# Expert rows modulated before they are stored, fetched and turned one expert at a time; six early weight loads wait for the first rows

## What is computed

```python
x = x + gate1 * (merged @ w_out[l])
h2 = rmsnorm(x, norm2_g[l]) * (1.0 + scale2) + shift2
x = x + gate2 * grouped_moe(h2, router_w, router_b, w_gate[l], w_up[l], w_down[l])

def grouped_moe(h, router_w, router_b, w_gate, w_up, w_down):
    # 16 experts in 4 groups; every token goes to 2 experts of its best group
    hidden = silu(einsum('td,edf->tef', t, w_gate)) * einsum('td,edf->tef', t, w_up)
    hidden = hidden * combine[:, :, None]
    y = einsum('tef,efd->td', hidden, w_down)
```

## Time and profile before

| engine | busy us | share of the span |
|---|---|---|
| PE | 767.5 | 90% |
| DVE | 606.0 | 71% |
| ACT | 478.0 | 56% |
| POOL | 105.0 | 12% |

### The profile page before, as it was taken

The page is one execution under the profiler, slowest core; times in us unless marked ns, Lnnn a source line. Parts: engine busy times, 40 slices in busy tenths (PEclk is TensorE's granted clock), DMA queues, the critical chain, the costliest instruction groups (busy, mean ns, idle before and its releaser), DMA issues.

```text
span 854.4 us, 10046 instructions
## 1 busy us (share of the span) xinstructions
PE 767.5 (90%) x3628; PEld 592.9 (69%) x3628; DVE 606.0 (71%) x800; ACT 478.0 (56%) x618; POOL 105.0 (12%) x87
## 2 busy tenths in 40 slices
PE   3799999999999889999999729899999899999883
PEld 2687787776666556678888627677878787878772
DVE  4686887425998875545772427789899989898980
ACT  6334224455656335554235517769697869687750
POOL 4020000000000000010000110022324131313111
PEclk9799999999999999999999858999999999999996
DMA  9919993111031111153373695999999999999613
GB/s 286 316 51 373 390 390 128 50 50 51 1 99 49 50 50 51 50 173 99 99 280 140 216 375 171 341 311 377 359 376 355 383 375 339 371 340 373 220 25 53
DMA packets 86875, 183.35 MB, mean 215 GB/s; under 512 B 8064, under 2 KB 27624, under 8 KB 84784
## 3 DMA queue, kind: packets, MB, share of 16 engines
q1 hardware_dynamic: 79200, 156.29, 50.3%
q0 software_dynamic: 7632, 26.52, 11.1%
HBM read 170.17 MB, written 12.62 MB: 214 GB/s over the span
## 4 chain that ended last, share of the span: by engine, by line
PE 63%; ACT 10%; issue 8%; DVE 8%; DMA 7%; POOL 1%; SPq 1%; ACTq 0%; POOLq 0%; DVEq 0%
PE ps L646 16%; PE ps L647 15%; PE ps L648 15%; PE ps L802 4%; DMA gx<-rows_scratch,slot_tok 3%; ACT w_hi L1433 3%; ACT hgT_hi L1460 3%; DMA out<-ys,slot_tok 2%; ACT hm L1466 2%; DMA raw<-in_w_in 1%; PE ps L784 1%; PE ps L886 1%; DVE w_lo L1538 1%; PE ps L902 1%; PE ps L914 1%
## 5 line engine op out<-in xcount | busy, mean ns | idle before, releaser
L1858 DVE TENSOR_TENSOR w_lo<-raw,w_hi 128x2048 fp32r<-128x2048 f32 x80 | 179.7, 2285 | 15.9 <-ACT w_hi L1433 15.9
L1433 ACT ACTIVATE w_hi<-raw 128x2048 fp32r<-128x2048 f32 x80 | 151.0, 1910 | 12.0 <-PE ps L648 12.0
L646 PE MATMUL ps<-w_lo,hgT_hi 128*128 128x512 f32 x256 | 106.8, 417 | 15.0 <-DVE hgT_lo L1963 14.9
L646 PE MATMUL ps<-act_lo,w_hi 128*128 128x512 f32 x232 | 98.7, 426 | 7.1 <-DVE act_lo L1580 3.1
L647 PE MATMUL ps<-w_hi,hgT_lo 128*128 128x512 f32 x256 | 104.8, 409 | 0.0
L648 PE MATMUL ps<-w_hi,hgT_hi 128*128 128x512 f32 x256 | 104.2, 407 | 0.0
L648 PE MATMUL ps<-act_hi,w_hi 128*128 128x512 f32 x232 | 91.4, 394 | 0.0
L647 PE MATMUL ps<-act_hi,w_lo 128*128 128x512 f32 x232 | 91.1, 393 | 0.0
L1168 ACT ACTIVATE w_hi<-raw 128x2048 fp32r<-128x2048 f32 (+2 forms) x29 | 51.9, 1794 | 67.3 <-DMA raw<-in_w_in 44.1
L1538 DVE TENSOR_TENSOR w_lo<-raw,w_hi 128x2048 fp32r<-128x2048 f32 (+2 forms) x29 | 61.9, 2145 | 31.7 <-ACT w_hi L1168 31.5
L646 PEld LDWEIGHTS ps<-w_lo,hgT_hi 128*128 128x128 f32 x256 | 51.0, 199 | 28.9 <-DVE hgT_lo L1963 17.9
(11 more groups left out here) (266 smaller groups left out, 1418.8 us busy)
## 6 DMA issues: line engine op xcount, KB each, us to landing
raw<-in_w_down SPq DMA_DIRECT2D x32, 1024.0 KB, 10.6
raw<-in_w_gate SPq DMA_DIRECT2D x30, 1024.0 KB, 10.4
raw<-in_w_up SPq DMA_DIRECT2D x18, 1024.0 KB, 9.7
raw<-in_w_in SPq DMA_DIRECT2D x16, 1024.0 KB, 6.4
raw<-in_w_ada SPq DMA_DIRECT2D x16, 1024.0 KB, 7.1
raw_late<-in_w_up SPq DMA_DIRECT2D x14, 1024.0 KB, 8.6
raw<-in_w_ada SPq DMA_DIRECT2D x8, 512.0 KB, 6.8
raw_early<-in_w_ada SPq DMA_DIRECT2D x8, 512.0 KB, 6.2
```

Of the source, the lines that this page charges most:

```text
L646: pe.matmul(o, a[0], b[1], start=start, stop=False)
L1433: act.activation(e_hi[s_][:, :], e_raw[r][:, :], ACT.Copy).then_inc(e_top, 1)
L1858: dve.tensor_tensor(e_lo[s_][:, :], e_raw[r][:, :], e_hi[s_][:, :].bitcast(F32), ALU.subtract).then_inc(e_split, 1)
```

## The change

Five things change together.

1. DVE makes the fully modulated row before it is stored. POOL loads three broadcast rows (amp2r from scale2, shift2r, and g2r, which waits until PE is done with ob1). `amp_row` makes amp once, `by_amp` multiplies the new xres by it half by half, and `modulated` multiplies by 1/rms and adds the shift. ACT's `rows_scaled` goes. So after the transposes the high part is a plain copy, and the low part a subtraction: hm and nsh2c go.
2. Rows are turned for one expert at a time, in every stage, after the four chunks and before `down`: eight transposes, two ACT copies of 128x512, two DVE subtractions of 128x512. Every stage waits for its own two halves before chunks 0 and 1. Each of the two gx buffers has its own semaphore.
3. At the start only expert 0 is turned before stage 0, and its index is made by itself (`singly`) before that of expert 1.
4. The loads z = 6 to 11 wait, besides what they waited for, until expert 0's rows have landed.
5. In stage 15 the first half of `down(14)` runs before `turn_hid(15)` and the second half after it, and hidT is split in two halves.

```diff
+                    if isinstance(z, int) and 6 <= z < E_RAW:
+                        sp.wait_ge(rows_in[0], 16)
...
+            for dst, src in ((amp2r, mod_d[1][:, 0:D]), (shift2r, mod_d[0][:, D:2 * D])):
+                pool.dma_start(dst[:, :], src.partition_broadcast(P).rearrange("p a d -> p (a d)")).then_inc(ld_rw2, 16)
+            pool.wait_ge(seg_ready, seg_done("ob1", 3))
+            pool.dma_start(g2r[:, :], norm2_g.partition_broadcast(P).rearrange("p a d -> p (a d)")).then_inc(ld_rw2, 16)
...
-                pool.wait_ge(idx_ok, X - X % 2 + 2)
+                pool.wait_ge(idx_ok, X + 1)
                 if X >= 2:
-                    pool.wait_ge(hg_ps, 2 * (X - X % 2))
+                    pool.wait_ge(hg_ps, 2 * X - 2)
                 pool.indirect_dma_start(gx[X % 2][:, :], None, rows_d,
                                         bass.IndirectOffsetOnAxis(slot_tok[:, X % N_EXP:X % N_EXP + 1], 0)
-                                        ).then_inc(rows_in, 16)
+                                        ).then_inc(rows_in[X % 2], 16)
...
-            def turn_rows(X, units):
-
-
-                for u in units:
-                    if u == 0:
-                        pe.wait_ge(rows_in, 16 * X + 32)
-                    if not isinstance(X, int) or X > 0 or u >= 2:
-                        pe.wait_ge(hg_sp, 2 * X + u - 1)
-                    for j in range(2):
-                        kk = 2 * u + j
-                        for b in range(2):
-                            last = pe.transpose(ps[2 + u % 2][:, P * (2 * j + b):P * (2 * j + b) + P],
-                                                gx[b][:, P * kk:P * kk + P], ident[:, :])
+            def turn_rows(X, b):
+
+                pe.wait_ge(rows_in[b], 8 * X + 16 - 8 * b)
+                if not isinstance(X, int) or X > 0:
+                    pe.wait_ge(hg_sp, 2 * X)
+                for u in range(2):
+                    for j in range(4):
+                        kk = 4 * u + j
+                        last = pe.transpose(ps[2 + u][:, P * j:P * j + P], gx[b][:, P * kk:P * kk + P], ident[:, :])
                     last.then_inc(hg_ps, 1)
...
+                    if singly and b:
+                        pe.wait_ge(sel_ready, X + 2)
+                        pe.wait_ge(idx_ok, X + 1)
...
-                    pe.wait_ge(hg_sp, 2 * X + 2)
+                pe.wait_ge(hg_sp, 2 * X + 1)
                 if not fresh:
                     pe.wait_ge(silu_ok, X)
                 up_chunk(X, 0, b, z0, z)
-                if b == 0:
-                    pe.wait_ge(hg_sp, 2 * X + 4)
+                pe.wait_ge(hg_sp, 2 * X + 2)
...
-                if b == 1 and not last_:
-                    turn_rows(X + 1, (0, 1))
+                if last_:
+                    down(X - 1, z0 + 4, z + 4, (0,))
+                    turn_hid(X)
+                    down(X - 1, z0 + 4, z + 4, (1,))
+                    return
+                turn_rows(X + 1, 1 - b)
...
-            def rows_scaled(tt):
-                act.wait_ge(h2_rs, tt + 1)
-                act.activation(hn[:, tt, :], xres[:, tt, :], ACT.Copy, scale=st[:, tt, 5:6]).then_inc(h2_rows, 1)
...
-            def hg_high(X, u):
-                act.wait_ge(hg_ps, 2 * X + u + 1)
-                for j in range(2):
-                    kk = 2 * u + j
-                    last = act.activation(hgT_hi[:, :, kk, :], ps[2 + u % 2][:, 2 * P * j:2 * P * j + 2 * P].rearrange(
-                        "p (b s) -> p b s", b=2), ACT.Identity, bias=sh2c[:, kk:kk + 1], scale=amp2c[:, kk:kk + 1])
-                last.then_inc(hg_hi, 1)
-                act.wait_ge(hg_hi, 2 * X + u + 1)
-                for j in range(2):
-                    kk = 2 * u + j
-                    last = act.activation(hm[:, :, kk, :], hgT_hi[:, :, kk, :].bitcast(F32), ACT.Identity,
-                                          bias=nsh2c[:, kk:kk + 1])
-                last.then_inc(hg_hm, 1)
+            def hg_high(X, b):
+                for u in range(2):
+                    act.wait_ge(hg_ps, 2 * X + u + 1)
+                    act.activation(hgT_hi[:, b, 4 * u:4 * u + 4, :], ps[2 + u][:, :].rearrange("p (k s) -> p k s", k=4),
+                                   ACT.Copy).then_inc(hg_hi, 1)
...
+                if not last_:
+                    hg_high(X + 1, 1 - b)
...
+            def amp_row():
+                dve.wait_ge(ld_rw2, 48)
+                dve.scalar_tensor_tensor(out=amp2r[:, :], in0=amp2r[:, :], scalar=1.0, in1=g2r[:, :], op0=ALU.add,
+                                         op1=ALU.mult).then_inc(amp_ok, 1)
+                dve.wait_ge(amp_ok, 1)
+
+            def by_amp(half, t0, t1):
+
+                a = slice(512 * half, 512 * half + 512)
+                dve.wait_ge(x1_ready, 4 * half + t1)
+                dve.tensor_tensor(hn[:, t0:t1, a], xres[:, t0:t1, a],
+                                  amp2r[:, a].unsqueeze(1).broadcast_to([P, t1 - t0, 512]), ALU.mult).then_inc(rows_amp, 1)
+
+            def modulated(tt):
+                dve.wait_ge(rows_amp, 2 + tt)
+                dve.wait_ge(h2_rs, tt + 1)
+                dve.scalar_tensor_tensor(out=hn[:, tt, :], in0=hn[:, tt, :], scalar=st[:, tt, 5:6], in1=shift2r[:, :],
+                                         op0=ALU.mult, op1=ALU.add).then_inc(h2_rows, 1)
...
-            def hg_low(X, u):
-                dve.wait_ge(hg_hm, 2 * X + u + 1)
-                for j in range(2):
-                    kk = 2 * u + j
-                    last = dve.scalar_tensor_tensor(
-                        out=hgT_lo[:, :, kk, :], in0=ps[2 + u % 2][:, 2 * P * j:2 * P * j + 2 * P].rearrange(
-                            "p (b s) -> p b s", b=2), scalar=amp2c[:, kk:kk + 1], in1=hm[:, :, kk, :], op0=ALU.mult,
-                        op1=ALU.subtract)
-                last.then_inc(hg_sp, 1)
+            def hg_low(X, b):
+                for u in range(2):
+                    dve.wait_ge(hg_hi, 2 * X + u + 1)
+                    dve.tensor_tensor(hgT_lo[:, b, 4 * u:4 * u + 4, :], ps[2 + u][:, :].rearrange("p (k s) -> p k s", k=4),
+                                      hgT_hi[:, b, 4 * u:4 * u + 4, :].bitcast(F32), ALU.subtract).then_inc(hg_sp, 1)
...
+                if last_ is not None:
+                    dve.wait_ge(hidT_h, X + 1)
+                    dve.tensor_tensor(hidT_lo[:, 0:2, :], ps[4][:, 0:2 * P].rearrange("p (k s) -> p k s", k=2),
+                                      hidT_hi[:, 0:2, :].bitcast(F32), ALU.subtract).then_inc(hidT_sp, 1)
+                    dve.wait_ge(hidT_h2, last_)
+                    dve.tensor_tensor(hidT_lo[:, 2:4, :], ps[4][:, 2 * P:4 * P].rearrange("p (k s) -> p k s", k=2),
+                                      hidT_hi[:, 2:4, :].bitcast(F32), ALU.subtract).then_inc(hidT_sp2, 1)
+                    return
```

More of the change, by code:

```diff
@@ L184, in hybrid_layer @@
     before = tiny("before", [P])
[L185 to L186 removed]
+    sc2c, sh2c, g2c, amp2c = (at(n, [KD], F32, small[0] + i / 32)
+                                     for i, n in enumerate(("sc2c", "sh2c", "g2c", "amp2c")))
     identb = tiny("identb", [P], BF16)
@@ L1067, in slot_table @@
                                          start=(tt == 0), stop=(tt == NT - 1))
-                last.then_inc(ws_ps, 2)
+                    if singly:
+                        last.then_inc(ws_ps, 1)
+                if not singly:
+                    last.then_inc(ws_ps, 2)
             def up_chunk(X, cc, b, z0, z):
@@ L1079, in up_chunk, with down @@
                 m.then_inc(e_used, 1)
-            def down(X, z0, z):
-                pe.wait_ge(hidT_sp, X + 1)
-                if not isinstance(X, int) or X > 0:
-                    pe.wait_ge(y_sb, 2 * X)
-                for h in range(2):
+            def down(X, z0, z, halves=(0, 1), rest=None):
+                if 0 in halves:
+                    pe.wait_ge(hidT_sp, X + 1)
+                    if not isinstance(X, int) or X > 0:
+                        pe.wait_ge(y_sb, 2 * X)
+                for h in halves:
+                    if h and rest is not None:
+                        pe.wait_ge(hidT_sp2, rest)
                     pe.wait_ge(e_split, z + h + 1)
@@ L1128, in stage, with expert_pass @@
                     slot_table(X + 2, e + 2)
-            def expert_pass(X0):
-                slot_table(X0, 0)
-                turn_rows(X0, range(4))
+            def expert_pass(X0, turn):
+                slot_table(X0, 0, True)
+                turn_rows(X0, 0)
                 stage(X0, 0, 0, True, False)
@@ L1139, in expert_pass @@
                 stage(X0 + N_EXP - 1, N_EXP - 1, 1, False, True)
-                down(X0 + N_EXP - 1, 10, EC * (X0 + N_EXP) - 2)
-            expert_pass(0)
+                down(X0 + N_EXP - 1, 10, EC * (X0 + N_EXP) - 2, (0, 1), turn)
+            expert_pass(0, 1)
             pe.wait_ge(route_ok, 1)
@@ L1502, in expert_pass @@
                         high_e(EC * X0 + cc, cc, Y0 + 1)
-                for u in range(4):
```

(18 more changed lines are left out.)

94 lines of the change are left out of this document (45 added, 49 removed).

## The result

The changed kernel takes 830.66 us (median of 4 runs, 826.92 to 832.38) where the kernel before took 853.06 on the same chip: ratio 0.973, 95% interval 0.967 to 0.979. That is 22.4 us less, inside the range given and 6 us short of the gain forecast.

A forecast was written before the change was run, and what follows sets the result against it. Prediction saw PE, DVE and DMA nearly full. PE/DVE terms 12.5 + 18.0 + 1.0 + 0.4 = 31.9 us, DMA at most 31.4; about 31.5 less 3 is 28.5, so 850.8 - 28.5 = 822 us, range 818 to 829.

The forecast's parts named there:

- Router phase: Before the ranking: added DVE work charged 1.3 us (0 to 3.0); building the first index for one expert gives 0.9 back.
- First rows: Expert 0's fetch to first expert matmul: 6.3 us from issue to landing, fewer turning steps, first matmul 7.5 us earlier.
- To expert 2: From the start to expert 2's second weight chunk: 12.5 us earlier in all, including the 7.5 at the first matmul.
- Each pair: Two experts' stages: hgT_lo wait goes, 37.3 us (36.6 to 39.5) instead of 40.3; six pairs give 18.0 us.
- DMA bound: Weight loads from 505 us: 109.1 MB at 372 GB/s, last landing at 798, at most 31.4 us gained.
- Interplay: Over the expert phase: two close limits each bite in turns, so 3 us taken off the gain.
- End: Last expert: split of down(14) and hidT gains 0.4 us; the last two experts lose the clock dip, 1.0.
- PE alone: Rival for the expert pairs: PE sets the pace, a pair takes 36.6 us, 815 in all; chance 0.14.
- The slow pairs: Rival: pairs stay near 40 us as DVE or loads replace the hgT_lo wait, 838 us; chance 0.18.
- The memory cap of 358 GB/s: Rival for the loads: memory gives no more than this fixed rate, 19.6 us gained, 831 us; chance 0.03.
- Starvation by held loads: Rival: the six later loads and all behind them delay the end, 872 us at 315 GB/s; chance 0.03.
- ACT waiting for weights: Sign expected toward the end of the kernel, for the first time; no size given.

The follow-up runs named there:

- hold four: The changed kernel with loads 8 to 11 held back instead of 6 to 11: ratio 0.971, median 827.6 us.
- tail whole: The changed kernel with down(14) in one piece and the last expert's hid converted in one piece behind it: ratio 0.973, median 828.5 us.
- turned behind down: The changed kernel with the next expert's rows turned behind the down product instead of ahead of it: ratio 1.008, median 858.2 us.
- hold two: The changed kernel with only loads 10 and 11 held back instead of 6 to 11: ratio 0.972, median 827.6 us.

## Why the prediction came out right, step by step

The sum for its own profile was 28.5 us and the two traces give 30.0 behind the residual. The timed gain is 22 to 23. Two things lie between. First, that profile of before was a slow specimen: against its second one it had one more fall of the clock (1.6 us) and, behind the first expert matmul, 2.5 us more of waiting for fetched rows (2.38 and 0.59 for 0.50), and it ended 4.1 us later behind the residual. I saw it stand 5.3 above the median, let that stand, and took the whole sum off the median all the same. The second profile of before, 850.9 us, is at the median, and its end of 410.3 leaves 25.7. Second, the later front: 3.3 us between the repeated profiles (442.11 and 438.82), 2.4 in the means, of which nothing could be forecast from the diff. 25.7 less 3.3 is the 22.4 us between those two executions.

The near hit of 28.5 on 30.0 is partly luck. At the second weight chunk of expert 2 the changed kernel is 14.1 us ahead (556.42 - 439.97 before, 548.36 - 446.04 now; 12.5 forecast), at that of expert 14 another 17.0 (18.0 forecast), and from there to the end it loses 1.2 (1.4 gain forecast). So the start was undersized and the end had the wrong sign. The three errors come to -2.0 us, which the 3 us taken off for interplay happened to cover, though they were meant for the pairs.

- *Router phase*, +1.3: the ranking is 1.0 later (46.8 for 45.8; 0.7 against the second profile). The direction is right. The single index gave 1.5 instead of 0.9, so that the fetch goes out 0.5 earlier (57.4 for 57.9) where +0.4 was forecast.
- *First rows*, -7.5: 10.7 measured. The step that failed is the 6.3 us from issue to landing, which measured 4.1 (to the transposes). I had the landing near 6 us with or without four loads beside it. Without the hold it was 8.5 (499.12 to 507.60). In this kernel the hold is worth 6.3 of the 10.7. Of the 2.2 us too many, 1.2 are the issue itself, which took 1.03 us and not the 2.23 that I took from before. The estimate from the Trainium skill (DMA: Bandwidth & Descriptors, Anatomy of one DMA), 3.2 us behind the issue, fits the trace: the issue ends at 504.47 and the transposes start 3.0 later.
- *To expert 2*, -12.5: 14.1. That is the 3.2 more of the step before, less 1.5 that PE waited for the third expert's rows at 538.73.
- *Each pair*, 37.3: it is 37.36. Before it was 40.2 on the mean of the six, not 40.3 each, so 2.8 us are gained and not 3.0, and 1.3 of them are clock. The pair before was 36.6 plus 2.1 of waiting plus 1.6 in 5 of 6 pairs; I saw 1.2 us a pair of clock, but did not tie it to the wait, and named a dip as a gain for the last two experts alone. The window of 40.2 us at clock 1.00 that I took for one pair holds more than one, as a pair at clock 1.00 takes 38.7: so its 37.8 of DVE was too much (34.7 to 37.9 in the six pairs, 36.2 on the mean). That the order covers hi and lo held: without the cover a pair costs 4.7 more (5.2 forecast). What keeps a pair from 36.6 is not the DVE, as I argued. DMA has a part in it: with 2 or 4 MB of loads done early the middle pairs fell to about 36.9, and PE's waits for gx from 2.3 us to 0.7 over the same 240 us (hold four). These waits are 0.3 us a pair, about half of what the middle pairs gained; the other half was not traced, nor was what keeps them above 36.6.
- *DMA bound*, last landing 798: it came at 791.6, 785.5 once the late front is taken off. The rate of 372 was mis-sized: 384 to 385 in the pairs and 412 before them. The way I had the bound bite, by the last weights pulling the end, did not come: by my own 11.3 us from the last landing to PE's end PE could have been through at 796.8, and it was at 810.6 (816.6 less 6.07). ACT waited for no weights up to the end. DMA is as full as the pairs want it (37.7 us for 14.68 MB at 389 GB/s), but what it costs here is the late landing of the fetched rows.
- *Interplay*, 3 off: the sum of the parts by PE and DVE was 31.9, the profile gave 30.0. The pairs fell short of their part by 1.0 only.
- *End*, 0.4 gained and 1.0 of clock: 1.2 lost. The split alone lost 1.0 (tail whole): the step that failed is that `turn_hid` now comes before silu is ready (1.47 us), and the second half of hidT still leaves PE 2.29 of waiting.
- *Rivals.* PE alone (815) failed by the 0.76 us a pair above 36.6, of which PE's waits for fetched rows are 0.4, and by the end. The slow pairs (838) did not come. The memory cap of 358 GB/s that the Trainium skill states without a condition (DMA: Bandwidth & Descriptors, its opening table) does not hold for this core by itself: the trace shows 384 over a whole pair. Starvation by held loads is there in small: 0.3 us a pair over all six, 0.5 in the middle four, paid back where fewer are held. ACT waiting for weights, which I named as a sign, did not show, neither between 545 and 785 us nor behind.

## What to carry to other kernels

Price a wait of the pacing engine with what it does to the clock: look for pairs of the same work at two lengths, and compare their granted clocks. A transfer that everything waits for should find the queues empty, so hold back bulk loads that would be in flight with it, but only those; each one more is a debt to a stretch in which DMA may be full. (Here the profiles show that debt, the timed medians do not resolve it.) Split a step only where the second part has something to cover: here the split tail, meant to save 0.4 us, cost 1.0.

## What was not expected of the hardware

A wait of 2.1 us on PE was followed in 9 of 12 cases by about 3 us at 1.2 GHz, beginning 0.1 to 1.5 us after work had resumed, and in 3 of 12 by nothing. Some thirty PE waits of up to 0.9 us (turned behind down) left the clock at 1.00. The same indirect fetch of 0.52 MB took 4.1 us from issue to the transposes behind it with no load beside it (5.2 in hold two) and 8.5 beside four 1 MB loads, and a row store of 0.52 MB beside four loads 11 us. The DMA share stood at 1.04 with 384, 389 and 412 GB/s alike, so the share alone does not tell whether the rate could rise; adding traffic told it.
